# Delta rule: levels 0 to 4 of a triangular inverse on packed 32x32 blocks instead of full 128x128 tiles

## The reference, cut to what matters

```
A   = strictly_lower( beta * (k @ k.T) * decay )      # 128 x 128
inv = (I + A) ** -1
u   = inv @ (beta * v)
w   = inv @ (k scaled by beta and decay)
```

## Time and profile before

| what | value |
|---|---|
| time, median of 3 runs (lowest, highest) | 1721.43 us (1715.71, 1722.75) |
| profiled execution: span from first to last instruction | 1712.1 us |
| its own total time | not listed apart; the median of the runs is 9.3 us over the span |
| TensorE matmul busy | 1668.7 us, 97% of the span |
| VectorE busy | 1029.0 us, 60% |
| ScalarE busy | 837.1 us, 49% |
| GpSimd busy | 167.0 us, 10% |
| mean granted TensorE clock, as a share of full speed | 0.997 |

### The profile page before, as it was taken

How to read it: one execution, slowest core, us unless ns; L and a number is a source line. 1 busy time by engine, 2 the same in 40 slices (tenths; PEclk the granted TensorE clock), 3 DMA queues, 4 the chain that set the end, 5 groups by cost and what they waited for, 6 DMA issues and landing times.

```text
span 1712.1 us, 24840 instructions
## 1 busy us (share of the span) xinstructions
PE 1668.7 (97%) x10188; PEld 1438.8 (84%) x10188; DVE 1029.0 (60%) x1307; ACT 837.1 (49%) x1209; POOL 167.0 (10%) x170
## 2 busy tenths in 40 slices
PE   9998999999998999999999999999999999989998
PEld 8996888888776788888888888889889999968886
DVE  5853247665636567656765576656766364666653
ACT  5553434554335455543654455535555354445542
POOL 0223510000000100010000130012000020020000
PEclk9999999999999999999999999999999999999999
DMA  8554158665477786656775666555445142676652
GB/s 259 174 171 149 51 163 257 190 185 196 147 269 239 249 241 180 193 176 171 197 200 192 185 172 192 177 197 172 137 134 173 50 147 88 203 235 179 186 192 89
DMA packets 329160, 306.37 MB, mean 179 GB/s; under 512 B 11953, under 2 KB 286934, under 8 KB 328918
## 3 DMA queue, kind: packets, MB, share of 16 engines
q1 hardware_dynamic: 324390, 296.71, 56.6%
q10 hardware_dynamic: 4384, 7.01, 1.1%
q0 software_dynamic: 272, 1.05, 0.2%
HBM read 303.69 MB, written 1.05 MB: 178 GB/s over the span
## 4 chain that ended last, share of the span: by engine, by line
PE 88%; DVE 4%; ACT 3%; issue 2%; POOL 1%; DMA 1%; SPq 0%; ACTq 0%; DVEq 0%; POOLq 0%
PE ps L445 22%; PE ps L497 17%; PE ps L435 15%; PE ps L448 10%; PE ps L516 8%; ACT whi L393 2%; PE ps L444 1%; DMA raw<-in_b_w_qkv 1%; PE ps L1921 1%; PE ps L1317 1%; PE ps L1301 1%; PE ps L2520 1%; DVE wlo L399 1%; PE ps L2419 1%; PE ps L536 1%
## 5 line engine op out<-in xcount | busy, mean ns | idle before, releaser
L399 DVE TENSOR_TENSOR wlo<-raw,whi 128x2048 fp32r<-128x2048 f32 x246 | 565.5, 2300 | 371.7 <-ACT whi L393 371.4
L445 PE MATMUL ps<-a_split,whi 128*128 128x512 f32 x1760 | 609.7, 399 | 5.2 <-DVE a_split L728 2.5
L393 ACT CAST whi<-raw 128x2048 fp32r<-128x2048 f32 x246 | 467.4, 1901 | 254.4 <-PE ps L497 154.1
L448 PE MATMUL ps<-a_split,wlo 128*128 128x256 f32 x1540 | 431.9, 280 | 0.0
L445 PEld LDWEIGHTS ps<-a_split,whi 128*128 128x128 f32 x1760 | 317.0, 188 | 69.6 <-issue 6.5
L448 PEld LDWEIGHTS ps<-a_split,wlo 128*128 128x128 f32 x1540 | 290.9, 189 | 10.5 <-issue 1.4
L435 PE MATMUL ps<-a_split,whi 128*128 128x256 f32 x1280 | 234.8, 286 | 0.0
L435 PEld LDWEIGHTS ps<-a_split,whi 128*128 128x128 f32 x1280 | 201.1, 193 | 0.8
L435 PE MATMUL ps<-a_split,wlo 128*128 128x256 f32 x640 | 181.6, 284 | 0.0
L497 PE MATMUL ps<-whi,fh 128*128 128x512 f32 x440 | 171.5, 390 | 0.0
L497 PE MATMUL ps<-whi,fl 128*128 128x512 f32 x440 | 171.2, 389 | 0.0
(11 more groups left out here) (376 smaller groups left out, 1879.1 us busy)
## 6 DMA issues: line engine op xcount, KB each, us to landing
raw<-in_f_w SPq DMA_DIRECT2D x132, 512.0 KB, 4.5
raw<-in_w_a SPq DMA_DIRECT2D x132, 512.0 KB, 4.4
raw<-in_w_ada SPq DMA_DIRECT2D x72, 512.0 KB, 4.4
raw<-in_w_in SPq DMA_DIRECT2D x68, 512.0 KB, 4.7
raw<-in_w_b SPq DMA_DIRECT2D x66, 512.0 KB, 4.4
raw<-in_a_w_in SPq DMA_DIRECT2D x32, 512.0 KB, 5.3
raw<-in_b_w_qkv SPq DMA_DIRECT2D x24, 512.0 KB, 6.1
raw<-in_a_w_out SPq DMA_DIRECT2D x8, 512.0 KB, 4.4
```

The source lines that it names most:

```text
L393: act.copy(whi[:, c % RING, :], raw[:, r % RING, :]).then_inc(S("hi_ready"), 1)
L399: dve.tensor_tensor(wlo[:, c % RING, :], raw[:, r % RING, :], whi[:, c % RING, :].bitcast(F32), ALU.subtract).then_inc(S("lo_ready"), 1)
L445: last = pe.matmul(o[:, :].rearrange("p (s t) -> p s t", s=2), wh[:, k, cols_], a_split[:, :, k, :], start=(k == 0), stop=(k == KD - 1))
L448: pe.matmul(o[:, 0:T], wl[:, k, cols_], ah[:, k, :], start=False, stop=False)
```

## The change

A packed form is used for levels 0 to 4, where all that matters lies in the four 32x32 blocks on the diagonal of each head. `unit_low` and `unit_c` hold these blocks for 8 heads as 128 partitions (block d, row) by 8x32 columns. For each chunk and level there is one step for all 8 heads:

- `unit_w_pe`: 8 matmuls with a stationary operand of 32 columns and 128 moving columns, each into one 32-partition quarter of the bank (at level 0 two transposes instead);
- ScalarE and VectorE copy it out negated, two instructions each of 32 partitions by 256 elements, into a block-diagonal `unit_w`;
- `unit_t_pe`, from level 1 on: two transposes of the packed inverse, and one VectorE copy;
- `unit_p_pe`: one matmul with the identity and 256 moving columns, which brings the old packed inverse into the bank, and 8 matmuls with 32-column stationary operands that add to it;
- ScalarE and VectorE copy the result into the diagonal blocks of the full `inv` (two instructions each, 32 partitions by 256), and ScalarE copies it to `unit_p` once all four are done.

`inv` and `unit_w` are set to zero once by POOL. The two chunks take turns, level by level. Levels 5 and 6 stay as they were, but invt now comes from a transpose of inv (`level_first_pe`), and the order of everything behind is new. The table in SBUF is 448 columns narrower; `inv` and `invt` change places in memory. Semaphore renames are left out below, as are the lines that only count differently.

```diff
+    def unit_low_act(act, tt):
+        act.wait_ge(*S("low", 4))
+        for d in (0, 1):
+            act.copy(unit_low[quad(d), tt, :, :], lowt[quad(d), tt, :, quad(d)]).then_inc(S(f"unit_low{tt}"), 1)
...
+    def unit_c_pool(pool, tt, s):
+        if s == 0:
+            pool.wait_ge(*S(f"unit_low{tt}", 4))
+        else:
+            pool.wait_ge(*S(f"unit_w_ps{tt}", s))
+        mask = tab("lev32", 5)[:, s, :].unsqueeze(1).to_broadcast([P, 8, 32])
+        pool.tensor_tensor(unit_c[:, tt, :, :], unit_low[:, tt, :, :], mask, ALU.mult)\
+            .then_inc(S(f"unit_c{tt}"), 1)
+    def unit_w_pe(pe, tt, s):
...
+            pe.wait_ge(*S(f"unit_inv{tt}", 4 * s))
+            for h in range(8):
+                g, q = h // HG, h % HG
+                last = pe.matmul(out[quad(q), g * P:g * P + P], unit_c[:, tt, h, :], inv[:, tt, h, :],
+                                 start=True, stop=True)
+    def unit_w_dve(dve, tt, s):
+        dve.wait_ge(*S(f"unit_w_ps{tt}", s + 1))
+        for q in (2, 3):
+            dve.tensor_scalar(*unit_w_rows(tt, q), -1.0, None, ALU.mult).then_inc(S(f"unit_w{tt}"), 1)
+    def unit_p_pe(pe, tt, s):
...
+        pe.matmul(out[:, 0:2 * P].rearrange("p (a b) -> p a b", a=8), ident, old, start=True, stop=False)
+        pe.wait_ge(*S(f"unit_w{tt}", 4 * s + 4))
+        if s:
+            pe.wait_ge(*S(f"unit_t{tt}", s))
+        for g in range(2):
+            for d in range(4):
+                left = unit_t[:, tt, g, d, :] if s else tab("id32")
+                last = pe.matmul(out[quad(d), g * P:g * P + P], left, unit_w[:, tt, g, d, :],
+                                 start=False, stop=(g == 1))
+        last.then_inc(S(f"unit_p_ps{tt}"), 1)
+    def unit_inv_act(act, tt, s):
+        act.wait_ge(*S(f"unit_p_ps{tt}", s + 1))
+        for d in (0, 1):
+            act.copy(*unit_inv_rows(tt, d)).then_inc(S(f"unit_inv{tt}"), 1)
+        if s < 4:
+            act.wait_ge(*S(f"unit_inv{tt}", 4 * s + 4))
+            act.copy(unit_p[:, tt, :, :], ps[UNIT_P[tt]][:, 0:2 * P].rearrange("p (a b) -> p a b", a=8))\
+               .then_inc(S(f"unit_p{tt}"), 1)
+    def unit_pe(pe, tt, s, between=lambda: None):
+        unit_w_pe(pe, tt, s)
+        if s:
+            unit_t_pe(pe, tt, s - 1)
+        between()
+        unit_p_pe(pe, tt, s)
+    def unit_dve(dve, tt, s):
+        unit_w_dve(dve, tt, s)
+        if s:
+            unit_t_dve(dve, tt, s - 1)
+        unit_inv_dve(dve, tt, s)
+    LEVELS = (5, 6)
     def gdn_pe(pe):
         for n in range(4):
             group_pe(pe, n)
+        for s in range(4):
+            unit_pe(pe, 0, s, lambda: ada_chunk_pe(pe, s))
+            unit_pe(pe, 1, s)
+        unit_pe(pe, 0, 4, lambda: ada_chunk_pe(pe, 4))
+        unit_w_pe(pe, 1, 4)
+        unit_t_pe(pe, 1, 3)
         for g in range(2):
             level_first_pe(pe, 0, g)
...
+        unit_p_pe(pe, 1, 4)
+        for g in range(2):
+            level_w_pe(pe, 0, 5, g)
+        ada_cols_pe(pe, 0)
+        for g in range(2):
+            level_first_pe(pe, 1, g)
+        for g in range(2):
+            level_yz_pe(pe, 0, 5, g)
+        ada_chunk_pe(pe, 5)
+        for g in range(2):
+            level_turn_pe(pe, 0, g)
+        ada_chunk_pe(pe, 6)
+        for g in range(2):
+            level_w_pe(pe, 0, 6, g)
+        ada_chunk_pe(pe, 7)
+        for g in range(2):
+            level_yz_pe(pe, 0, 6, g)
+        for g in range(2):
+            level_w_pe(pe, 1, 5, g)
         ada_cols_pe(pe, 1)
         for g in range(2):
+            level_yz_pe(pe, 1, 5, g)
+        for g in range(2):
+            first_u_pe(pe, g)
+        for g in range(2):
+            level_turn_pe(pe, 1, g)
+        for g in range(2):
+            first_s_pe(pe, g)
+        for g in range(2):
+            level_w_pe(pe, 1, 6, g)
+        for g in range(2):
+            first_o_pe(pe, g)
+        for g in range(2):
+            level_yz_pe(pe, 1, 6, g)
+        second_qs_pe(pe)
         second_uw_pe(pe)
+        for g in range(2):
+            turned_pe(pe, g)
+        for g in range(2):
+            second_v_pe(pe, g)
         ada_chunk_pe(pe, 8)
...
         ada_chunk_pe(pe, 9)
         for g in range(2):
             second_o_pe(pe, g)
```

More of the change, by code:

```diff
@@ L934, in build @@
     erow = at("erow", 76, [P, HG, P])
-    inv = at("inv", 8, [P, 2, 8, P])
+    invt = at("invt", 8, [P, 2, 8, P])
+    unit_w = at("unit_w", 16, [P, 2, 2, 4, P])
+    unit_p = at("unit_p", 32, [P, 2, 8, 32])
+    unit_t = at("unit_t", 34, [P, 2, 2, 4, 32])
     vn = at("vn", 16, [P, 2, 8, P])
@@ L943, in build @@
     g_osq = gbf[:, 1024:2048].rearrange("p (g a b) -> p g a b", g=2, a=HG)
-    g_o, g_wt = inv, lowt
+    g_o, g_wt = invt, lowt
+    unit_low = gbf[:, 1024:1536].rearrange("p (t a b) -> p t a b", t=2, a=8)
+    unit_c = gbf[:, 1536:2048].rearrange("p (t a b) -> p t a b", t=2, a=8)
     ba = sm(32).rearrange("p (t c) -> p t c", t=2)
@@ new lines, in unit_low_dve, with unit_zero_pool @@
+    def unit_low_dve(dve, tt):
+        dve.wait_ge(*S("low", 4))
+        for d in (2, 3):
+            dve.tensor_copy(unit_low[quad(d), tt, :, :], lowt[quad(d), tt, :, quad(d)]).then_inc(S(f"unit_low{tt}"), 1)
+    def unit_zero_pool(pool):
+        pool.wait_ge(*S("kv_ps", 4))
+        for tt in range(TT):
+            pool.memset(unit_w[:, tt, :, :, :], 0.0).then_inc(S("w_zero"), 1)
+    def unit_c_pool(pool, tt, s):
[6 more added lines that the diff above has]
+            .then_inc(S(f"unit_c{tt}"), 1)
@@ new lines, in unit_p_pe @@
+    def unit_p_pe(pe, tt, s):
+        out = ps[UNIT_P[tt]]
+        if s == 0:
+            pe.wait_ge(*S("low", 4))
+            pe.wait_ge(*S("att", 4))
+            pe.wait_ge(*S("vbeta", 4))
+            pe.wait_ge(*S("kdg", 4))
+            old = tab("id32").unsqueeze(1).to_broadcast([P, 8, 32])
+        else:
+            pe.wait_ge(*S(f"unit_p{tt}", s))
+            old = unit_p[:, tt, :, :]
+        pe.matmul(out[:, 0:2 * P].rearrange("p (a b) -> p a b", a=8), ident, old, start=True, stop=False)
[8 more added lines that the diff above has]
+        last.then_inc(S(f"unit_p_ps{tt}"), 1)
@@ new lines, in unit_inv_dve, with unit_t_pe @@
+    def unit_inv_dve(dve, tt, s):
+        dve.wait_ge(*S(f"unit_p_ps{tt}", s + 1))
+        if s == 0:
+            dve.wait_ge(*S("inv_zero", 1))
+        for d in (2, 3):
+            dve.tensor_copy(*unit_inv_rows(tt, d)).then_inc(S(f"unit_inv{tt}"), 1)
+    def unit_t_pe(pe, tt, s):
+        pe.wait_ge(*S(f"unit_p{tt}", s + 1))
+        for g in range(2):
+            last = pe.transpose(ps[UNIT_T[tt]][:, g * P:g * P + P], flat(unit_p[:, tt, heads(g), :]), ident)
+        last.then_inc(S(f"unit_t_ps{tt}"), 1)
@@ L1289, in level_first_pe, with step, first_bank @@
+    def unit_dve(dve, tt, s):
[4 more added lines that the diff above has]
+    LEVELS = (5, 6)
+    def step(tt, s, g):
+        return 4 * tt + 2 * (s - 5) + g
+    def first_bank(tt, g):
+        return ((0, 4), (2, 5))[tt][g]
+    def level_first_pe(pe, tt, g):
+        pe.wait_ge(*S(f"unit_inv{tt}", 20))
         for h in range(HG):
-            last = pe.transpose(bank(g, HG)[:, h, :], invt[:, tt, HG * g + h, :], ident)
+            last = pe.transpose(bank(first_bank(tt, g), HG)[:, h, :], inv[:, tt, HG * g + h, :], ident)
@@ L1555, in gdn_pe @@
         for g in range(2):
             second_v_pe(pe, g)
+        ada_chunk_pe(pe, 8)
         ada_chunk_pe(pe, 9)
@@ L1635, in gdn_pool @@
             group_pool(pool, n)
+        unit_zero_pool(pool)
+        for s in UNITS:
+            for tt in range(TT):
+                unit_c_pool(pool, tt, s)
         for tt in range(TT):
-            for s in range(7):
+            for s in LEVELS:
                 for g in range(2):
                     level_pool(pool, tt, s, g)
-                if tt and s == 4:
-                    norm_pool(pool, 0)
-                    norm_pool(pool, 1)
+        norm_pool(pool, 0)
+        norm_pool(pool, 1)
         norm_pool(pool, 2)
```

284 lines of the change are left out of this document (145 added, 139 removed), and 4 rows, old and new, of the table TAKES_OVER.

## The result

The changed kernel takes 1695.15 us (median of four runs, 1693.22 to 1697.50) against 1720.84 us of the kernel before on the same chip (median of four): a ratio of 0.9856, 95% interval 0.9836 to 0.9875. The prediction was 1700.0 us with a range of 1692 to 1715 and faster at 0.8; time and sign came as forecast, 5 us better than the point.

The account below looks back on a forecast made before the run. TensorE was taken to bound the stage. Packed levels of 6.2 us instead of 13.3 and the walk behind them ended it at 215.6, not 237.4: 21.8 us off span 1712.1 gave 1690.3, plus 9.3, so 1700 us, range 1692 to 1715.

Parts of the forecast that it names:

- TensorE holds 88%: Whole delta rule stage: TensorE holds 88% of what ended last, so time saved there is saved at the end.
- The half-level, 2.83 and 3.3 us: Packed levels: VectorE's copies set one half, TensorE with an ada chunk the other; a level 6.2 us, not 13.3.
- The product of 16 packed instructions: W and P products of the packed levels: taken as 0.83 us, bounds 0.65 and 2.05.
- rival 3: Packed products: quarters do not overlap, 2.05 us for 0.83, a level 9.9, 18.5 us more, 1718; chance 0.04.
- VectorE's copies: Copies out of PSUM in each half-level: five, 0.33 us apart, 1.75 us in all; bounds 0.27 to 0.69 apart.
- rival 1: Packed levels: copies 0.6 us apart from strides or waits, a level 8.2, 10 us more, 1709.6; chance 0.13.
- Lag and hand-back: Packed half-level: 0.10 us from the end of a matmul to the copy, 0.15 from copy to TensorE.
- The walk behind the levels: Full products after the last packed P: TensorE again the bound, groups of 1.86 us, g_out stream starting at 215.6.
- a sign of error on my own list: End of the stage: idle time before ada 11 or the last turns was listed as showing the forecast wrong.
- The runs' median is 9.3 us above that span, and I carry this over: Final step: 9.3 us added to the forecast span of 1690.3, giving 1699.6, so 1700 us.
- Rival 2: Clock low through all packed levels after 3.3 us idle: a level 9.3, 15.5 us more, 1715; chance 0.12.
- rival 4: Low clock goes on through 43 us of full products: up to 36 us more, 1751, slower than before; chance 0.04.

Follow-up runs that it names:

- run 3: Changed kernel plus two unused VectorE copies in each of the first eight half-levels, one contiguous on 32 partitions, one in blocks on 128; 1700.15 us.
- run 1: Changed kernel with the five ada chunks moved from between the packed levels to behind them; 1706.03 us.
- Runs 1 and 2: run 1, and three runs adding unused copies to the changed kernel: one VectorE (1697.08 us), two wide VectorE (1707.55), one ScalarE (1700.27).
- run 7: Changed kernel reordered level by level: both chunks' W products, then both P products, then the ada chunk; 1690.72 us, 0.9839 to the kernel before.
- run 6: The changed kernel again, no edit; 1697.12 us, 0.9873 to the kernel before.
- Run 5: Kernel before, with the new order but without the packing, full products in all six levels; 1707.68 us, ratio 0.994 to the kernel before.
- second run of 2: Changed kernel plus two unused contiguous 128-partition VectorE copies of 256 elements in each of the first eight half-levels; 1707.55 us.
- run 4: Changed kernel with the chunks no longer taking turns: five packed levels of chunk 0, then those of chunk 1; 1709.31 us.

## Why the prediction was right

**The bound.** "TensorE holds 88%, so time saved on its way through the stage is saved at the end": right, but for 1.3 us at the qkv weights and 0.7 near 1466.

**The half-level, 2.83 and 3.3 us.** The level of 6.2 us came to the hundredth (6.20), and that is luck: both halves take 3.10, one 0.27 more than its sum and the other 0.2 less, with terms wrong in opposite directions:

- The product of 16 packed instructions, taken as 0.83 for its starts: it took 0.65, the value that columns give. The quarters run side by side, also where they accumulate; rival 3 is out.
- VectorE's copies, taken as 0.33 apart and 1.75 for five: they are 0.46 apart and take 2.25 (153.08 to 155.33). ScalarE's, taken as 0.27 apart, take 0.39. That is what rival 1 named, slow copies, at two fifths of its price (0.5 us a half in place of 1.25), and by another mechanism: not strides, but copies that do not overlap (run 3). My bounds, 0.27 to 0.69, held it. The rows I took were near in elements, but their neighbours overlap by 0.08, and these don't.
- Lag and hand-back, 0.10 and 0.15: 0.05 and 0.14. Sum 0.65 + 0.05 + 2.25 + 0.14 = 3.09.
- The ada chunk "sets that half" at 3.3: it does not (run 1). With it TensorE is full but not late, since P costs 0.2 less than I took, and the copies set both halves alike.

**Copies, not the array, set the level.** Runs 1 and 2 show it. The Trainium skill's warning ("TensorEngine Tiling (Array Packing)", Performance Considerations) that packing does not speed up the emptying of PSUM agrees with these traces. They are copies out of PSUM, with the hand-overs around them. The limit was not the last word, though: run 7 hides the hand-overs by order alone, 1.34 us a level.

**The walk behind the levels.** Last P forecast 171.3 to 172.1, measured 170.97; v 205.3, measured 204.35; ada 11 loaded at 212.6, measured start 212.28 behind 1.14 us of DMA wait, the wait that I had named as the next one, and a sign of error on my own list; stream 215.6, measured 214.52. The groups of 1.86 were 1.79 apiece, as here:

```profile
190.76 1.95 PE L1540 MATMUL ps<-vn,kdg 128*128 128x128 f32 x16
192.54 1.95 PE L1468 MATMUL ps<-inv,x 128*128 128x128 f32 x16
...
196.12 1.95 PE L1483 MATMUL ps<-invt,x 128*128 128x128 f32 x16
198.05 2.02 PE L1578 MATMUL ps<-state,qkv 128*128 128x128 f32 x16
```

Only q times state waits (1.93 us after YZ, not 1.79), as forecast. POOL and the moved norm and split cost nothing.

**"The runs' median is 9.3 us above that span, and I carry this over":** the step that failed. A run stands 1.8 us above its own span. The rest was the luck of the profiled execution: with 1712.1 + 1.8 it lay under all three runs shown, and it lost 3.4 us of clock time behind the stage where the changed kernel lost 6.8 and 10.2. The forecast of the span, 1690.3, was 4.5 low (the stage 1.1 better; the clock 3.4, the qkv weights 1.3 and the wait near 1466 0.7 worse); the median was 4.9 lower than the forecast. So part of the hit is luck: the span came out 4.5 too high for the forecast and the step from span to median 7.5 too low, and what remained was within the range. Later comparisons had the kernel before at 1713.78 to 1722.41 us.

**Rival 2, the low clock.** Its trigger was real and my argument against it ("3.22 of idle time did no harm") rested on one execution. Seven of nine had the low clock, but for 3.5 to 10 us. In run 6 it cost the stage 1.7 us, and not the 15.5 of a clock low through all levels; rival 4's low clock through the full products never came. (Its 36 us were low for what it describes: 43 us of TensorE work at half the clock take 43 more.) The prediction also read from the earlier trace rows that the clock came back when only transposes had run. That happened again in run 7's execution (16 transposes from 1488.08 on, the clock back near 1491.6), but not in run 6's, where it came back near 1504.2, with the second eight of these transposes and two ada chunks between. What the page "TensorE: Matmul & The Clock Gate" of the Trainium skill says of transposes, Part 4, no run here tested in the packed levels: packed products ran beside the transposes in each of these stretches.

**What brought the gain** the prediction left in one sum. Run 5 divides it: 9.7 us the order, 10.6 us more the packing on top of it, of 20.3 on that chip. The stage's ends, each with the estimate of its low clock taken off, say some 9 and 13. So "its matmuls run back to back", said of a level before, was wrong by 1.4 us a level, and the prediction had no rival in which the order alone gains. That the total of the stage came out within 1.1 us does not depend on it, since the new level was added up from its own terms.

## What to carry to other kernels

Once small products run side by side, the copies out of PSUM set the pace: count them per engine, price them by a row whose neighbours follow each other in the same way (from one quarter of the partitions to the next, or not), and choose the order in which none of these engines waits for the other's hand-over (level by level beat taking turns by 1.34 us a level). Test a new order without the new arithmetic before giving the arithmetic the credit; busy time contains stops, so it doesn't bound what an order can win. An execution's clock luck is worth several microseconds here: compare stage ends in the trace, sum the low-clock time, and put independent work into an idle time ahead of a dense stage.

## What the runs showed of the hardware that was not expected

- VectorE copies of 256 elements that start in another quarter of the partitions than the one before do not overlap with it: 0.42 to 0.43 us long and 0.45 to 0.46 apart, on 32 partitions and on 128 (changed kernel, run 7). Neighbours that start in the same quarter overlap by 0.08 us (second run of 2, and `cell` in the kernel before).
- Sixteen products with 32-column stationary operands, 128 rows and 128 columns take 0.64 to 0.65 us at full clock and 1.08 at the low clock.
- Behind 3.2 to 3.5 us without TensorE work the granted clock went to 0.50 (1.2 GHz) in seven of nine executions and stayed at 1.00 in two, and in the profiled one before; with idle times of at most 1.3 us it stayed in three of three.
- The clock also fell inside packed levels where TensorE waited for more of each half: in run 4 at 173.8 us, behind 10 us with TensorE busy for 5.2; in run 3 at 163.7, behind 10 us with 5.8; in the second run of 2 at 165.2, behind 10.2 us with 6.3. In run 1 it held through 10 us with 6.1. What decides the runs don't tell.
